# Router logits from unnormed residual rows, affinity turn ahead, second gate and row turns beside the sort

## What is computed

```python
x = x + gt1 * (jnp.concatenate([att, conv], axis=-1) @ w_out[l])
h2 = modulate(rmsnorm_2(x, g_ffn[l]), sh2, sc2)        # h*(1+sc2)+sh2
x = x + gt2 * expert_choice_ffn(h2, w_router[l], w_gate[l], w_up[l], w_down[l])
...
aff = jax.nn.softmax((h @ w_router).astype(jnp.float32), axis=-1)   # 16 experts
g, idx = lax.top_k(jnp.swapaxes(aff, 1, 2), cap)                    # cap = 128 tokens
xs = jax.vmap(lambda hb, ib: hb[ib])(h, idx)
y = (silu(xs @ w_gate) * (xs @ w_up)) @ w_down * g     # per expert
out = jax.ops.segment_sum(y, idx)                       # back to tokens
```

## Time and profile before

| | us |
|---|---|
| median of 3 runs | 2589.52 |
| lowest, highest | 2587.97, 2590.65 |
| the profiled execution | 2590.66 |
| its span (first to last instruction) | 2588.8 |
| TensorE busy | 2452.7 (95%) |
| DVE, ACT, POOL busy | 1610.7, 1254.0, 689.7 |

### The profile page before, as it was taken

How to read it: one execution, slowest core, us unless ns; L and a number is a source line. 1 busy time by engine, 2 the same in 40 slices (tenths; PEclk the granted TensorE clock), 3 DMA queues, 4 the chain that set the end, 5 groups by cost and what they waited for, 6 DMA issues and landing times.

```text
span 2588.8 us, 32543 instructions
## 1 busy us (share of the span) xinstructions
PE 2452.7 (95%) x11378; PEld 1918.5 (74%) x11378; DVE 1610.7 (62%) x2439; ACT 1254.0 (48%) x1852; POOL 689.7 (27%) x396
## 2 busy tenths in 40 slices
PE   8999899999999999999999999999997999999996
PEld 5787567777778788777778777765764888888884
DVE  5032887756643367665432635588247999999997
ACT  4121554434543323343433421376344888888886
POOL 1222100113434477334456222121220110111100
PEclk9999999999999999999999999999998999999997
DMA  7100000022222264222223111000138999999996
GB/s 279 49 33 17 34 1 1 1 114 82 82 82 97 97 230 146 80 82 84 95 98 114 66 65 49 33 1 1 67 117 316 402 387 386 397 386 390 396 361 219
DMA packets 86601, 384.06 MB, mean 148 GB/s; under 512 B 7980, under 2 KB 9180, under 8 KB 71520
## 3 DMA queue, kind: packets, MB, share of 16 engines
q1 hardware_dynamic: 81744, 365.25, 37.5%
q0 software_dynamic: 4752, 17.43, 2.5%
HBM read 361.60 MB, written 21.05 MB: 148 GB/s over the span
## 4 chain that ended last, share of the span: by engine, by line
PE 72%; issue 11%; DVE 8%; POOL 4%; ACT 4%; DMA 1%; POOLq 0%; SPq 0%; DVEq 0%; ACTq 0%
PE ps L947 10%; PE ps L949 10%; PE ps L948 10%; PE ps L1299 7%; PE ps L1301 7%; PE ps L1300 7%; POOL w_lo L2667 4%; PE ps L756 3%; PE ps L902 2%; PE ps L826 2%; PE ps L828 2%; PE ps L827 2%; PE ps L748 2%; PE ps L1149 1%; PE ps L770 1%
## 5 line engine op out<-in xcount | busy, mean ns | idle before, releaser
L2667 POOL TENSOR_TENSOR w_lo<-arena,w_hi 128x1024 fp32r<-128x1024 f32 x188 | 462.7, 2462 | 746.4 <-ACT w_hi L1544 742.2
L2543 DVE TENSOR_TENSOR e_lo<-arena,e_hi 128x1024 fp32r<-128x1024 f32 x384 | 454.2, 1221 | 45.4 <-ACT e_hi L1875 34.1
L1875 ACT ACTIVATE e_hi<-arena 128x1024 fp32r<-128x1024 f32 x384 | 404.1, 1062 | 103.1 <-PE ps L1301 103.1
L1544 ACT ACTIVATE w_hi<-arena 128x1024 fp32r<-128x1024 f32 x188 | 198.4, 1055 | 362.9 <-PE ps L949 362.9
L947 PE MATMUL ps<-h_hi,w_hi 128*128 128x512 f32 x848 | 342.6, 404 | 21.4 <-POOL w_lo L2667 11.7
L948 PE MATMUL ps<-h_lo,w_hi 128*128 128x512 f32 x848 | 335.9, 396 | 0.0
L949 PE MATMUL ps<-h_hi,w_lo 128*128 128x512 f32 x848 | 335.9, 396 | 0.0
L947 PEld LDWEIGHTS ps<-h_hi,w_hi 128*128 128x128 f32 x848 | 162.9, 192 | 66.1 <-issue 28.1
L1299 PE MATMUL ps<-e_hi,x_hi 128*128 128x512 f32 x512 | 202.2, 395 | 3.0 <-DVE x_lo L2538 2.6
L1301 PE MATMUL ps<-e_lo,x_hi 128*128 128x512 f32 x512 | 199.5, 390 | 0.0
L1300 PE MATMUL ps<-e_hi,x_lo 128*128 128x512 f32 x512 | 199.3, 389 | 0.0
(11 more groups left out here) (372 smaller groups left out, 5094.4 us busy)
## 6 DMA issues: line engine op xcount, KB each, us to landing
arena<-in_w_up SPq DMA_DIRECT2D x108, 1024.0 KB, 7.0
arena<-in_w_down SPq DMA_DIRECT2D x86, 1024.0 KB, 7.2
arena<-in_w_gate SPq DMA_DIRECT2D x64, 1024.0 KB, 9.4
arena<-in_w_in SPq DMA_DIRECT2D x18, 1024.0 KB, 4.8
arena<-in_w_out SPq DMA_DIRECT2D x16, 1024.0 KB, 4.7
arena<-in_w_ada SPq DMA_DIRECT2D x12, 1024.0 KB, 12.1
arena<-in_w_ada SPq DMA_DIRECT2D x24, 512.0 KB, 6.8
routed_rows<-arena SPq DMA_DIRECT2D x8, 520.0 KB, 2.6
```

What stands on the lines that cost most here:

```text
L1544: act_e.activation(w_hi[:, q, :], slot[c][:, q * D:(q + 1) * D], ACT.Copy).then_inc(s_whi, 1)
L1875: act_e.activation(e_hi[:, (2 * sl + a) % RING, :], slot[sl][:, a * D:(a + 1) * D], ACT.Copy).then_inc(s_ehi, 1)
L2543: v.tensor_tensor(e_lo[:, r, :], slot[sl][:, a * D:(a + 1) * D], e_hi[:, r, :].bitcast(F32), ALU.subtract).then_inc(s_elo, 1)
L2667: gp.tensor_tensor(w_lo[:, q, :], slot[c][:, q * D:(q + 1) * D], w_hi[:, q, :].bitcast(F32), ALU.subtract).then_inc(s_wlo, 1)
```

## The change

- **Logits from x.** wr_scaled is the router weight times the norm gain (DVE, once). The products take xT tiles of 128 tokens as stationary operand and 16 columns of wr_scaled as moving one, so that logits come out as rows. For the first half four groups of eight, for the second eight groups of four, one per k, summed over k by DVE. A further group of eight gives the shift's part (logits_shift). DVE multiplies by the inverse root and adds that part (affinity_shifted); hT isn't needed. The ACT copy and `logit_rows` are gone.
- **Place.** They stand inside projection items 9 to 14 and behind 15. `mean(13)` comes ahead of the row turns, `spread(13)` behind the affinity turns; root(13) is followed by the exponential.
- **Rows.** The order is h tiles 0 to 3, then all eight x tiles, then h tiles 4 to 7; four turns now lie ahead of the last item's end (were eight), on one pair of banks. There are three tok buffers.
- **Second half of h.** POOL multiplies xT by the inverse root (new, eight 128x512), ACT applies scale and shift in one operation each, between row copies 6 to 11.
- **Second gate.** Its weights move to slots 6, 10, 11 and a free region; no DVE preparation. Products of k = 0 to 5 alternate with row turns 6 to 11, k = 6 and 7 stand between position products in place of the fills. The DVE add moves behind expert 0's first eight e_lo.
- **Loads.** SP issues gate2 and expert weights in pieces between the row stores.

```diff
-        tok = [view(34, ROW), view(38.5, ROW)]
+        tok = [view(34, ROW), view(38.5, ROW), view(43, ROW)]
...
+        gate2_w = [view(192, ITEM), slot[6], slot[10], slot[11]]
...
         def row_bank(j):
 
-            return (4 if j < 8 else 0) + 2 * (j % 2)
+            return 4 if j < 4 else 2 * (j % 2)
+
+        def rows_kept(b):
+
+            return 16 * len(range(b, 2 * NT, 3))
 
         def row_tile(j):
 
-            return (j // 4) % 2, 4 * (j // 8) + j % 4
+            if j < 4:
+                return 1, j
+            return (0, j - 4) if j < 12 else (1, j - 8)
...
                 if g == 1:
...
-                if g == KT - 2:
-                    store_row(0)
-            for j in range(1, 8):
+                if g == 3:
+                    sp.dma_start(gate2_w[0].rearrange("p (a n) -> p a n", a=2), wga[0][:, :, 5 * D:6 * D]).then_inc(wl[8], 16)
+            for j in range(4):
...
             sp.wait_ge(tps, 2 * (T_OUT2 + 8))
-            expert_weights(0, 0)
-            for j in range(8, 10):
-                store_row(j)
-            sp.wait_ge(s_hb, 5 * KT)
-            for i in range(4):
-                sp.dma_start(slot[8 + i].rearrange("p (a n) -> p a n", a=2), wga[i][:, :, 5 * D:6 * D]).then_inc(wl[8 + i], 16)
-            for j in range(10, 2 * NT):
+            for i in range(1, 4):
+                sp.dma_start(gate2_w[i].rearrange("p (a n) -> p a n", a=2), wga[i][:, :, 5 * D:6 * D]).then_inc(wl[8 + i], 16)
+            for j in range(2):
+                expert_weights(0, 0, None, (2 * j, 2 * j + 1))
+                store_row(4 + 2 * j)
+                store_row(5 + 2 * j)
+            expert_weights(1, 0, None, (3,))
+            for j in range(8, 2 * NT):
                 store_row(j)
             sp.dma_start(gt2B, T["b_ada_2"][:, 5 * D:6 * D].to_broadcast([P, D])).then_inc(s_late, 16)
             sp.dma_start(g_fin, T["g_final_2"].rearrange("(a d) -> a d", a=1).to_broadcast([P, D])).then_inc(s_late, 16)
-            for b in range(2):
-                sp.wait_ge(s_tkst[b], 16 * NT)
+            for b in range(3):
+                sp.wait_ge(s_tkst[b], rows_kept(b))
             expert_weights(1, 0, None, range(2))
             sp.wait_ge(s_g2, 1)
-            expert_weights(1, 0, None, range(2, 4))
-            sp.wait_ge(s_gat[0], 16)
-            expert_weights(2, 0)
+            expert_weights(1, 0, None, (2,))
+            expert_weights(2, 0, None, range(2))
+            sp.wait_ge(s_g2, 2)
+            expert_weights(2, 0, None, range(2, 4))
             expert_weights(0, 1, 0)
...
-                if 2 <= j < 8 or j >= 10:
+                if 1 <= j < 4:
+                    pe.wait_ge(s_rte, j)
+                if j >= 6:
                     pe.wait_ge(s_rte, j - 1)
-                if j == 1:
-                    pe.wait_ge(s_rs, 13)
-                if j == 5:
-                    pe.wait_ge(s_aff, 1)
+                if h:
+                    pe.wait_ge(s_hb, (4 + j // 8) * KT)
                 for k in range(KT):
...
+            def logits_shift():
+
+                pe.wait_ge(s_wr, 1)
                 for k in range(KT):
-                    pe.wait_ge(s_hb, (3 + half) * KT + k + 1)
-                    m = pe.matmul(ps[0:NE, 7, :], wr[:, k, :], hT[:, k, half * HALF:(half + 1) * HALF], start=(k == 0), stop=(k == KT - 1))
-                m.then_inc(s_lg, 1)
-
-            def logit_rows(half):
-
-                pe.wait_ge(s_lgc, half + 1)
+                    pe.matmul(ps[:, 7, 4 * NE:5 * NE], mod[:, 24 + k, 0:1].to_broadcast([P, P]), wr[:, k, :], start=(k == 0), stop=(k == KT - 1))
+
+            def first_logits(i):
+
+                if i == 0:
+                    logits_shift()
+                    pe.wait_ge(evv, T_OUT2 + 4)
+                    pe.wait_ge(eva, T_OUT2 + 4)
+                for k in range(KT):
+                    m = pe.matmul(ps[:, 7, i * NE:(i + 1) * NE], xT[:, k, i * P:(i + 1) * P], wr_scaled[:, k, :], start=(k == 0), stop=(k == KT - 1))
+                if i == 3:
+                    m.then_inc(s_lg, 1)
+
+            def second_logits(k):
+
+                pe.wait_ge(eva if k % 2 else evv, T_OUT2 + 4 + k // 2 + 1)
+                if k == 0:
+                    pe.wait_ge(s_rm, 1)
                 for i in range(4):
-                    t = 4 * half + i
-                    m = pe.transpose(ps[:, 6, i * NE:(i + 1) * NE], lgT[:, t * P:(t + 1) * P], ident[0:NE, 0:NE])
-                m.then_inc(s_lg, 1)
+                    c = (4 * k + i) * NE
+                    m = pe.matmul(ps[:, 7, c:c + NE], xT[:, k, (4 + i) * P:(5 + i) * P], wr_scaled[:, k, :], start=True, stop=True)
+                if k == KT - 1:
+                    m.then_inc(s_lg, 1)
 
             for i in range(KT):
                 output_part2(i)
             output_part2(KT, {4: lambda: mean(12)})
-            output_part2(KT + 1, {2: lambda: spread(12)})
-            for i in range(2):
-                output_part2(KT + 2 + i, {1: lambda: row_turn(2 * i), 5: lambda: row_turn(2 * i + 1)})
-            output_part2(KT + 4, {0: lambda: logits(0), 6: lambda: logit_rows(0)})
-            output_part2(KT + 5, {5: lambda: row_turn(4)})
-            output_part2(KT + 6, {1: lambda: row_turn(5), 5: lambda: row_turn(6)})
-            output_part2(KT + 7, {1: lambda: row_turn(7)})
+            output_part2(KT + 1, {2: lambda: spread(12), 4: lambda: first_logits(0), 6: lambda: first_logits(1)})
+            output_part2(KT + 2, {1: lambda: first_logits(2), 4: lambda: first_logits(3)})
+            output_part2(KT + 3, {2: lambda: second_logits(0), 5: lambda: second_logits(1)})
+            output_part2(KT + 4, {2: lambda: second_logits(2), 6: lambda: row_turn(0)})
+            output_part2(KT + 5, {2: lambda: second_logits(3), 6: lambda: row_turn(1)})
+            output_part2(KT + 6, {2: lambda: second_logits(4), 6: lambda: row_turn(2)})
+            output_part2(KT + 7, {3: lambda: row_turn(3)})
+            for k in range(5, KT):
+                second_logits(k)
+            mean(13)
             pe.wait_ge(evv, T_OUT2 + 8)
             pe.wait_ge(eva, T_OUT2 + 8)
-            row_turn(8)
-            pe.wait_ge(s_rte, 8)
-            mean(13)
-            spread(13)
-            row_turn(9)
-            logits(1)
-            row_turn(10)
-            logit_rows(1)
-            row_turn(11)
+            row_turn(4)
+            row_turn(5)
 
             pe.wait_ge(s_aff, 2)
             for r in range(2):
...
+            spread(13)
+
+            def second_gate(k):
+
+                if k == 0:
+                    pe.wait_ge(s_rs, 14)
+                    pe.wait_ge(s_aff, 3)
                 if k % 2 == 0:
                     loaded("gate2", 8 + k // 2, 0)
                 for c in range(2):
-                    m = pe.matmul(ps[:, 2 + c, :], silu_b[:, k, :], slot[8 + k // 2][:, (k % 2) * D + c * 512:(k % 2) * D + (c + 1) * 512],
+                    m = pe.matmul(ps[:, 6 + c, :], scT[:, k, 0:1].to_broadcast([P, P]), gate2_w[k // 2][:, (k % 2) * D + c * 512:(k % 2) * D + (c + 1) * 512],
                                   start=(k == 0), stop=(k == KT - 1))
-            m.then_inc(s_g2, 1)
+                if k in (3, KT - 1):
+                    m.then_inc(s_g2, 1)
+
+            for k in range(6):
+                row_turn(6 + k)
+                second_gate(k)
+            for j in range(12, 2 * NT):
+                row_turn(j)
...
             squares(13, lambda k: xT[:, k, hi], lambda k: gated(KT + k),
-                    {1: lambda: (row_out(0), row_out(1), output2_high(KT + 4)), 2: lambda: (row_out(2), row_out(3), output2_high(KT + 5)),
-                     3: lambda: (logits_copied(0), router_exp(0), output2_high(KT + 6)), 4: lambda: (row_out(4), output2_high(KT + 7)),
-                     5: lambda: (row_out(5), row_out(6)), 6: lambda: row_out(7)})
+                    {1: lambda: output2_high(KT + 4), 2: lambda: output2_high(KT + 5), 3: lambda: (router_exp(0), output2_high(KT + 6)),
+                     5: lambda: (row_out(0), output2_high(KT + 7)), 6: lambda: row_out(1), 7: lambda: row_out(2)})
+            row_out(3)
             root(13)
-            row_out(8)
-            row_out(9)
+            act_e.activation(apad[:, 0:1], epst, ACT.Exp)
+            router_exp(1)
+            row_out(4)
+            row_out(5)
             spread(13)
-            shift_half(1, range(KT))
-            act_e.activation(apad[:, 0:1], epst, ACT.Exp)
-            logits_copied(1)
-            router_exp(1)
-            for j in range(10, 2 * NT):
+            for k in range(KT):
+                if k < 6:
+                    row_out(6 + k)
+                act_e.wait_ge(s_hp, k + 1)
+                act_e.activation(hT[:, k, hi], hT[:, k, hi], ACT.Identity, bias=mod[:, 24 + k, 0:1], scale=gsc[:, 2, k:k + 1]).then_inc(s_hb, 1)
+            for j in range(12, 2 * NT):
                 row_out(j)
...
+            def affinity_shifted(half):
+
```

(33 more changed lines are left out.)

98 lines of the change are left out of this document (41 added, 57 removed).

## The result

The changed kernel takes 2604.40 us (median of 4 executions, 2602.02 to 2606.39) beside 2588.74 for the kernel before; the ratio is 1.0053 with a 95% interval of 1.0038 to 1.0068. Measured again later, beside other runs of the kernel before, it was 2603.26 and 1.0051 (1.0036 to 1.0067). Forecast was 2590.5 in a range of 2582.5 to 2597.5. The profiled execution spans 2601.1 us, 12.3 more than the one before, and took 2602.93.

The account below looks back on a forecast made before the run. Whatever precedes the first expert product was taken to bound, with rows late behind the position table. Terms +6.3, -16.1, 0 in the sort and +10.8 behind it gave net +1.0, so 2590.5 us, range 2582.5 to 2597.5.

Parts of the forecast that it names:

- What bounds, and where to look: Whatever happens before the first expert product shifts the end one for one, and nothing after it matters.
- Part 1: Up to the last projection product: 15.4 us removed from TensorE's queue, 21.7 added, net +6.3, last product at 1943.1.
- Rival (B): The early half is cheap, small products at 0.1 or no clock fall: 4 to 8 us less, 2584; chance 0.10.
- Part 2: From the last projection product to the sort: falls from 24.7 to 8.6 us, sort at 1951.7.
- rival (D): POOL's eight 128x512 multiplies hold the sort: +4 us, 2593.5; chance 0.07.
- Part 3: Row copies wait on stores behind loads: last store at 1989.4, rows 8 us behind the position table.
- Rival (A): Rows don't bind, as the store queue drains faster or turns fit between: 9 us less, 2581; chance 0.13.
- Part 4: To the first expert: gather lands at 1996.4, first expert product at 2002.7 against 2001.69, +1.0 us.
- Rival (C): Beside the sort, row turns and gate steps alternate with waits at TensorE's low clock: +6 to +9 us, 2598; chance 0.15.

Follow-up runs that it names:

- both front edits: Changed kernel with the narrow product groups set apart and the first half's logits in a PSUM bank of their own: 2589.34 us, 1.0003 to the kernel before.
- own bank: Changed kernel with the first half's logits and the shift in a PSUM bank of their own: 2593.70 us, 1.0024 to the kernel before.
- all, filled: Changed kernel with narrow groups apart, own logits bank, row stores first, up loads behind the gather and more fills: 2582.51 us, 0.9974 to the kernel before.

## Why the prediction was wrong, step by step

**What bounds, and where to look.** Right. From the first expert product on the two profiles differ by 0.8.

**Part 1, up to the last product: the step that failed.** Forecast was +6.3, measured +12.5. Four of its terms hold: a narrow product at full clock takes 0.21 (16 records in 1.7), the wait for DVE's first logits 4.55 (forecast 4.7), the row turns 2.0 (2.5), the clock behind the wait 2.6 (2.0). Missing is a whole term: the clock falls a first time, in a row of 16 narrow products (8 for the shift, 8 for the first group), and costs 4.9. The forecast asked of TensorE's clock only what idle time does to it, as the row with 2.94 idle showed it, and counted a stretch without idle at full clock. Its 12.5 for 60 narrow products was a price at full clock that these products themselves don't leave standing. Two small terms were off as well. What was removed measures 14.8 and not 15.4, mainly since four row turns are 3.1 and not 3.6. And the first projection pass behind a narrow group takes 0.32 and not 0.23; all passes together are 0.5 longer in the kernel with both front edits than before. The terms as measured make 12.5 + 4.55 + 2.0 + 2.6 + 4.9 + 0.5 = 27.1 added, 14.8 removed: +12.3, beside +12.5. Rival (B), a cheap early half, is out by the same numbers.

**Part 2, to the sort.** Right: 8.6 forecast, 8.3 measured.

**The sort, rival (D).** Nothing came of it: MAX8 0.43 beside POOL's multiplies, 26.5 from start to table.

**Part 3, rows late.** Right in mechanism and size. Moved by the 6.1 that Part 1 was short and the 0.45 of the later mean(12), the forecast had row_out(9) freed at 1978.2, row_out(11) at 1984.7 and the last copy ended at 1993.2; measured are 1978.75, 1983.63 and 1993.6. The two kernels with another order of stores show that this is what bound: the table at 109.6 and 109.5 as in the changed kernel, the first expert product 0.6 and 6.5 earlier. Rival (A), that rows don't bind, is out.

**Part 4, to the first expert: a term mis-sized.** The last store was given 2.7 and took 4.62; the gather was given 6.1 and took 9.71. The 2.7 was read from a store that landed alone; the last one of the kernel before, with the same stores around it, took 4.7. And the 6.1 of the gather was taken with two up loads issued 2 to 3 us ahead of it. From the kernel before, the store issued at 1972.6 to 1973.3 and the loads of 1983 to 1990 (the last number is the time from issue to landing, a median for two):

```profile
routed_rows<-arena SPq DMA_DIRECT2D x1, 520.0 KB, 4.7
```

```profile
arena<-in_w_up SPq DMA_DIRECT2D x2, 1024.0 KB, 6.3
```

The changed kernel has three up loads 0.8 us ahead of the gather and the down loads right behind it. The forecast followed SyncE's queue to the last store and gave the loads behind it nothing, though the diff ahead of it shows them. Holding these loads back brought 5.14. The Trainium skill ("DMA: Bandwidth & Descriptors", "Queues, rings and completion order") says that a DMA engine takes turns between the queues that have work for it, packet by packet; the trace agrees in so far as the gather, on POOL's queue, was slower by 4.6 us with SyncE's loads beside it and still landed ahead of the last of them. Towards the other side, the counts on ACT, forecast to end about 3 us behind the gather's landing (1999 to 2000 against 1996.4), ended 4.2 ahead of it (2004.56 against 2008.73), so that 4.4 and not 6.3 lay between landing and first product. The sum of this part was 24.5 in the forecast and is 28.8.

**The sum.** +12.5, -16.4, 0 and +15.0 (28.8 less 13.75) are +11.1, as the positions have it (138.4 less 127.4); with the 0.45 of the later mean(12) and 0.8 behind, the 12.3 of the spans.

**Rival (C)**, slower by TensorE's clock, had the right engine and the wrong place: shares of 0.66 and 0.87 stand beside the sort, but the rows were later there. The chance of 0.25 for slower lay mostly on it.

**Range.** 2597.5 was its upper end. The first expert product was forecast at 128.4 and came at 138.4; the fall of the clock (4.9) and the excess of Part 4 (4.3, 28.8 less 24.5) are 9.2 of these 10.0 us. Without them 2604.4 would be 2595.2, inside the range.

## What to carry to other kernels

Price narrow products not by their own time alone: set them apart between wide ones, a few at a time, and look at the clock share of a stretch even where the engine shows no idle time. When a change makes one result earlier, list what else its first reader waits for; here the positions came 16 us earlier relative to the projection and waited for rows. And before a transfer is given a duration, take the row of the same transfer in the same place, not that of a lone one, and look at which loads the new order issues just around it on other queues.

## Hardware behaviour not expected

- TensorE's clock fell from 2.4 to 1.2 GHz while the engine was busy 2.00 us of 2, in a row of 16 products of 16 columns, in the changed kernel and, where the same number was added, in the kernel before (32 records, 4.19 us). Groups of 8 with two or more projection steps between them didn't do it. All seven profiles with that row of 16 in the projection show the fall.
- Such a fall isn't certain. A row of 12 such products and 4 with one column, behind the projection, dropped the clock in eight profiles and not in three.
- In six profiles with the same front the first fall lasted about fourteen passes, in the one that writes another bank six. Why isn't known.
- A gather of 128 rows took 5.14 us with the up and down loads held back, and 8.6 to 9.7 with three or four up loads of 1 MB issued around it and the down loads behind them (own bank: 8.74). With up and down loads held back but two gate loads issued less than 4 us ahead of it, it took 8.1 (all, filled).
